# One more seven-product gate/up group ahead of the pairs, in place of a plain one, in a two-layer encoder on one core

## What is computed

```python
x = x + 0.5 * swiglu(rmsnorm(x, norm_ffn), w_gate, w_up, w_down)      # D_FF = 2816

def swiglu(h, w_gate, w_up, w_down):
    return (jax.nn.silu(h @ w_gate) * (h @ w_up)) @ w_down
```

## Time and profile before

| | us |
|---|---|
| Median of 3 runs | 2633.71 (2633.64 to 2634.29) |
| The profiled execution, its own time | 2634.64 |
| Its span in the trace | 2632.8 |
| TensorE busy | 2619.0 (99% of the span) |
| VectorE busy | 1881.9 (71%) |
| ScalarE busy | 1097.5 (42%) |
| GpSimd busy | 239.9 (9%) |
| The 16 DMA engines, main queue | 31.8% of the span |

### The profile page before, as it was taken

The page is one execution under the profiler, slowest core; times in us unless marked ns, Lnnn a source line. Parts: engine busy times, 40 slices in busy tenths (PEclk is TensorE's granted clock), DMA queues, the critical chain, the costliest instruction groups (busy, mean ns, idle before and its releaser), DMA issues.

```text
span 2632.8 us, 38540 instructions
## 1 busy us (share of the span) xinstructions
PE 2619.0 (99%) x14658; PEld 2306.5 (88%) x14658; DVE 1881.9 (71%) x2462; ACT 1097.5 (42%) x1561; POOL 239.9 (9%) x143
## 2 busy tenths in 40 slices
PE   8999999999999999999999999999999999999999
PEld 6899998888888888999988999888888888889998
DVE  8788865564665467888878888664755644689887
ACT  5343444454543233443433434444544522333333
POOL 2512100000000000211001111000000000001110
PEclk9999999999999999999999999999999999999999
DMA  7433233233224333333223332432322333324331
GB/s 239 124 104 96 80 128 101 81 93 95 83 66 144 100 106 99 111 113 104 88 81 112 96 104 71 153 92 64 115 82 80 100 116 98 115 80 137 96 96 56
DMA packets 293325, 269.70 MB, mean 102 GB/s; under 512 B 14036, under 2 KB 272513, under 8 KB 292685
## 3 DMA queue, kind: packets, MB, share of 16 engines
q1 hardware_dynamic: 288072, 259.09, 31.8%
q0 software_dynamic: 4512, 5.04, 0.7%
q10 hardware_dynamic: 646, 4.31, 0.4%
HBM read 259.75 MB, written 13.28 MB: 104 GB/s over the span
## 4 chain that ended last, share of the span: by engine, by line
PE 89%; DVE 5%; issue 2%; ACT 2%; DMA 1%; POOL 0%; SPq 0%; DVEq 0%; ACTq 0%; POOLq 0%
PE proj L574 22%; PE proj L576 22%; PE proj L575 22%; PE acc L574 6%; PE acc L575 6%; PE acc L576 6%; DVE ring_lo L1566 1%; ACT ring_hi L1111 1%; PE acc L844 1%; DVE xs L1592 1%; DVE work L1733 1%; DMA raw<-in_ffn_down 1%; PE acc L783 0%; DVE y_lo L1596 0%; DVE work L1580 0%
## 5 line engine op out<-in xcount | busy, mean ns | idle before, releaser
L574 PE MATMUL proj<-h_hi,ring_hi 128*128 128x512 f32 (+1 forms) x1664 | 572.1, 344 | 0.9 <-DVE work L1620 0.8
L576 PE MATMUL proj<-h_hi,ring_lo 128*128 128x512 f32 (+1 forms) x1664 | 567.2, 341 | 0.0
L575 PE MATMUL proj<-h_lo,ring_hi 128*128 128x512 f32 (+1 forms) x1664 | 566.8, 341 | 0.0
L574 PE MATMUL proj<-y_hi,ring_hi 128*128 128x256 f32 (+1 forms) x1376 | 427.1, 310 | 0.0
L576 PE MATMUL proj<-y_hi,ring_lo 128*128 128x256 f32 (+1 forms) x1376 | 426.8, 310 | 0.0
L575 PE MATMUL proj<-y_lo,ring_hi 128*128 128x256 f32 (+1 forms) x1376 | 426.7, 310 | 0.0
L574 PEld LDWEIGHTS proj<-h_hi,ring_hi 128*128 128x128 f32 x1664 | 316.1, 190 | 37.2 <-issue 1.7
L1111 ACT ACTIVATE ring_hi<-raw 128x1024 fp32r<-128x1024 f32 (+1 forms) x175 | 223.9, 1281 | 299.1 <-PE acc L576 210.5
L576 PEld LDWEIGHTS proj<-h_hi,ring_lo 128*128 128x128 f32 x1664 | 315.8, 190 | 35.7
L575 PEld LDWEIGHTS proj<-h_lo,ring_hi 128*128 128x128 f32 x1664 | 316.2, 190 | 33.7
L1566 DVE TENSOR_TENSOR ring_lo<-raw,ring_hi 128x1024 fp32r<-128x1024 f32 (+1 forms) x176 | 296.6, 1688 | 48.7 <-ACT ring_hi L1111 48.2
(11 more groups left out here) (276 smaller groups left out, 3876.3 us busy)
## 6 DMA issues: line engine op xcount, KB each, us to landing
raw<-in_ffn_gate SPq DMA_DIRECT2D x88, 512.0 KB, 3.9
raw<-in_ffn_up SPq DMA_DIRECT2D x88, 512.0 KB, 4.2
raw<-in_w_in SPq DMA_DIRECT2D x136, 256.0 KB, 3.6
raw<-in_w_in SPq DMA_DIRECT2D x60, 512.0 KB, 4.7
raw<-in_ffn_down SPq DMA_DIRECT2D x56, 512.0 KB, 4.4
work<-in_ffn_down SPq DMA_DIRECT2D x32, 512.0 KB, 6.1
raw<-in_w_out SPq DMA_DIRECT2D x16, 512.0 KB, 4.1
raw<-in_w_ret_o SPq DMA_DIRECT2D x12, 512.0 KB, 3.8
```

The costliest lines, as they stand in the source:

```text
L574: pe.matmul(o, s_hi, m_hi, start=start, stop=False)
L575: pe.matmul(o, s_hi, m_lo, start=False, stop=False)
L576: return pe.matmul(o, s_lo, m_hi, start=False, stop=stop)
```

## The change

Only groups 0 and 1 stay plain. Group 2 becomes a seven-product group by itself (the *odd* group) that runs directly after the down product of group 0, with ring slots 4, 5, 0, 1, 4, 5, 0, while slots 2 and 3 are kept for down weights; the down product of groups 1 and 2 follows it (`down_odd`). The operand sums and all seven operand splits move ahead of it, the residual adds of down 0 and `ups(1, 6)` move behind them on VectorE, and TensorE waits for both plain up tiles' scaling before the first product, as the products use all four `PB` banks. GpSimd starts its differences one group sooner. The load of the second down weights goes to its own place and waits for the last operand split. In every fast group, odd or in a pair, the last three products now accumulate in PSUM on top of the first ones in their banks: two VectorE additions (`gate_lo`, `v_sum`) and one ScalarE copy (`c5_copy`) fall away, product 6 waits for the third sum in place of the copy, and the next group's product 0 waits for the low silu product, which reads the bank directly. Pairs are still four, of groups 3 to 10.

```diff
 GRP = 256
 GROUPS = D_FF // GRP
-PLAIN = 3
+PLAIN = 2
 ITEMS_PAIR, TILES_PAIR = 2 * PROD + 2, 2 * PROD + 8
-PAIR_ITEM, PAIR_TILE = 3 * PLAIN, 4 * PLAIN + 16
+ODD_ITEM, ODD_TILE = 5, 16
+OP_ORDER = (S1, S3, N2, S4, A11, A12, A22)
 PRODUCTS = ((0, A11), (1, S1), (3, S3), (2, N2), (0, A12), (3, A22), (1, S4))
+ADDED = 4
...
-                after(5)
-                whole(0, 3)
-                after(6)
-                whole(1, 3)
-                after(7)
-                down_rows(l, f, 2)
+                sp.wait_ge(op_lo_ready, 7 * (2 * l + f) + 7)
+                down_rows(l, f, 2, 1)
+                for piece, which, half in ((1, 0, 0), (2, 1, 0), (5, 0, 1), (6, 1, 1)):
+                    after(ODD_ITEM + piece)
+                    gate_up(l, f, which, half, 3)
...
+                first = ffn_item(l, f) + LO_CREDIT + ODD_ITEM
                 if F4 == 0:
                     pool.wait_ge(decay_out, 16)
                 else:
-                    pool.wait_ge(weights_lo, I0)
-                for n in range(FAST):
-                    edges(n, I0 + ITEMS_PAIR * ((n - 1) // 2) + PROD * ((n - 1) % 2))
+                    pool.wait_ge(weights_lo, first)
+                edges(0, 0)
+                edges(1, first)
+                for n in range(2, FAST):
+                    edges(n, I0 + ITEMS_PAIR * ((n - 2) // 2) + PROD * (n % 2))
...
+                def group(F, item, slots, bank3_free, bank2_free):
+                    free = ((silu_lo_ready, F + FREE), (c12_done, F + FREE), bank3_free, bank2_free,
+                            (c1_copied, F + 1), (u3_done, F + 1), (c22_done, F + 1))
+                    for j, (bank, op) in enumerate(PRODUCTS):
+                        pe.wait_ge(*free[j])
+                        product(item + j, slots[j], PB[bank], op, j >= ADDED)
...
+                    group(F, I, slots[:PROD], (ffn_x, 8 * added + 6), (ffn_x, 8 * added + 5))
+                    group(F + 1, I + PROD, slots[PROD:], (c21_done, F + 1 + FREE), (u2_done, F + 1 + FREE))
                     down_pair(I + 2 * PROD, i, 2)
...
-                gate(5, 4, 2)
-                split_done(6)
-                up(0, 2, 0)
-                up(0, 2, 1)
-                down_two(7, 1, 1, 2)
-                pe.wait_ge(op_lo_ready, 7 * F4 + 7)
-                pe.wait_ge(ffn_x, 8 * (DOWNS * F4 + 2) + 6)
+                pe.wait_ge(gate_scaled, 2 * (c0 + 1) + 4)
+                pe.wait_ge(up_scaled, 2 * (c0 + 1) + 4)
+                for j, (bank, op) in enumerate(PRODUCTS):
+                    pe.wait_ge(op_lo_ready, 7 * F4 + OP_ORDER.index(op) + 1)
+                    if j >= ADDED:
+                        pe.wait_ge((c1_copied, u3_done, c22_done)[j - ADDED], FAST * F4 + 1)
+                    product(ODD_ITEM + j, ODD_SLOTS[j], PB[bank], op, j >= ADDED)
...
                 sigmoids(1)
-                whole(0, 2, 4, 6)
+                odd_hi(0, 6)
                 for n, op in enumerate((S1, S3, N2, S4)):
                     operand_hi(op, (s_ready, 4 * F4 + n + 1))
-                whole(1, 2, 0, 8)
+                odd_hi(1, 6)
+                for op in (A11, A12, A22):
+                    operand_hi(op, (tiles_done, T0 + 8 + FIRST_CREDIT))
+                odd_hi(2, 8)
+                odd_hi(3, 8)
                 hidden_his(1)
-                down_hi(1, 2, 16)
-                sigmoids(2)
-                down_hi(2, 4, 18)
-                hidden_his(2)
-                for op in (A11, A12, A22):
-                    operand_hi(op, (tiles_done, T0 + 20 + FIRST_CREDIT))
-                piece_hi(0, 0, 0, -8)
-                piece_hi(0, 0, 1, -8)
+                F, q = FAST * F4, g0 + PLAIN
+                act.wait_ge(gated_ready, 2 * (c0 + 2))
+                c1_copy(F, ODD_TILE)
+                odd_hi(4, ODD_TILE + 1)
+                odd_hi(5, ODD_TILE + 2)
+                odd_hi(6, ODD_TILE + 3)
+                down_hi(1, ODD_TILE)
+                sigmoid_lo(F, q, ODD_TILE)
+                second_hi(1, ODD_TILE + 6)
+                sigmoid_hi(F)
+                hidden_hi(q, 1, 0)
+                hidden_hi(q, 1, 1)
+                pair_hi(0, 0, 0, -8)
+                pair_hi(0, 0, 1, -8)
...
+                def sums(F, tile):
+                    done(T0 + tile + 3)
+                    dve.wait_ge(c1_copied, F + 1)
+                    dve.tensor_tensor(u2, c1, PB[2][:, :], ALU.add).then_inc(u2_done, 1)
+                    dve.wait_ge(u2_done, F + 1 + FREE)
+                    dve.tensor_tensor(u3, u2, PB[3][:, :], ALU.add).then_inc(u3_done, 1)
+                    dve.wait_ge(u3_done, F + 1)
+                    dve.tensor_tensor(c22, u3, PB[1][:, :], ALU.add).then_inc(c22_done, 1)
+
+                def gate_hi(F, tile):
+                    done(T0 + tile + 5)
+                    dve.wait_ge(c22_done, F + 1)
+                    dve.tensor_tensor(c21, u2, PB[3][:, :], ALU.add).then_inc(c21_done, 1)
+
+                def silu_low(F):
+                    dve.wait_ge(sig_lo_ready, F + 1)
+                    dve.tensor_tensor(silu_lo, PB[0][:, :], silu_lo, ALU.mult).then_inc(silu_lo_ready, 1)
...
+                def up_lo(F, tile):
+                    done(T0 + tile + 6)
+                    dve.wait_ge(c21_done, F + 1 + FREE)
+                    dve.tensor_tensor(c12, u2, PB[1][:, :], ALU.add).then_inc(c12_done, 1)
...
-                    def sums(g):
-                        F = FAST * F4 + 2 * i + g
-                        done(T0 + B + PROD * g + 3)
-                        dve.wait_ge(c1_copied, F + 1)
-                        dve.tensor_tensor(u2, c1, PB[2][:, :], ALU.add).then_inc(u2_done, 1)
-                        dve.wait_ge(u2_done, F + 1 + FREE)
-                        dve.tensor_tensor(u3, u2, PB[3][:, :], ALU.add).then_inc(u3_done, 1)
-                        dve.wait_ge(c5_copied, F + 1)
-                        dve.wait_ge(u3_done, F + 1)
-                        dve.tensor_tensor(v_sum, u2, c5, ALU.add).then_inc(v_done, 1)
-                        dve.wait_ge(v_done, F + 1)
-                        dve.tensor_tensor(c22, u3, c5, ALU.add).then_inc(c22_done, 1)
-
-                    def gate_lo(g):
-                        done(T0 + B + PROD * g + 4)
-                        dve.wait_ge(u2_done, FAST * F4 + 2 * i + g + 1 + FREE)
-                        dve.tensor_tensor(c11, c1, PB[0][:, :], ALU.add).then_inc(c11_read, 1)
-
...
@@ -1736,46 +1750,55 @@
                 ups(0, 2)
                 lo(4, 2, 2048, raw[:, 2, :])
                 gates(1, 4)
-                lo(5, 4, 2048, raw[:, 0, :])
+                F, q = FAST * F4, g0 + PLAIN
                 dve.wait_ge(xn_ready, 8 * (F4 + 1))
                 dve.tensor_tensor(s_acc, xn21, xn22, ALU.add).then_inc(s_ready, 1)
                 dve.wait_ge(s_ready, 4 * F4 + 1)
                 dve.tensor_tensor(xn21, xn11, xn21, ALU.subtract).then_inc(s_ready, 1)
                 operand_lo(0, S1)
                 dve.tensor_tensor(s_acc, xn11, s_acc, ALU.subtract).then_inc(s_ready, 1)
-                add_down(0, 8, 0)
                 operand_lo(1, S3)
-                add_down(0, 8, 1)
                 dve.wait_ge(s_ready, 4 * F4 + 3)
                 operand_lo(2, N2)
-                add_down(0, 8, 2)
                 dve.tensor_tensor(s_acc, xn12, s_acc, ALU.add).then_inc(s_ready, 1)
-                add_down(0, 8, 3)
-                lo(6, 0, 2048, raw[:, 1, :])
-                for m in range(4, 6):
-                    add_down(0, 8, m)
+                odd_lo(0)
                 dve.wait_ge(s_ready, 4 * F4 + 4)
                 operand_lo(3, S4)
-                for m in range(6, KT):
-                    add_down(0, 8, m)
-                ups(1, 6)
-                lo(7, 2, 2048, raw[:, 2, :])
-                gates(2, 16)
-                lo(8, 4, 2048, raw[:, 2, :])
-                ups(2, 18)
+                odd_lo(1)
                 operand_lo(4, A11)
                 for m in range(4):
-                    add_down(1, 20, m, PLAIN_BANKS)
+                    add_down(0, 8, m)
                 operand_lo(5, A12)
                 operand_lo(6, A22)
-                add_down(1, 20, 4, PLAIN_BANKS)
+                add_down(0, 8, 4)
+                add_down(0, 8, 5)
+                t2(F)
+                add_down(0, 8, 6)
+                odd_lo(2)
+                add_down(0, 8, 7)
+                odd_lo(3)
+                t4(F, q)
+                ups(1, 6)
+                for j in (4, 5, 6):
+                    odd_lo(j)
+                sums(F, ODD_TILE)
+                lo(ODD_ITEM + PROD, 2, 2048, raw[:, 2, :])
+                silu_low(F)
+                gate_hi(F, ODD_TILE)
+                hidden_hi(F, q)
+                lo(ODD_ITEM + PROD + 1, 4, 2048, down_second)
+                up_lo(F, ODD_TILE)
+                hidden_lo(F)
+                y_low(q, 1, 0)
+                y_low(q, 1, 1)
                 piece_lo(0, 0, 0)
                 piece_lo(0, 0, 1)
```

(61 more changed lines are left out.)

239 lines of the change are left out of this document (100 added, 139 removed).

## The result

The changed kernel takes **2715.42 us** (median of 6 runs, 2714.16 to 2718.48) against 2633.74 (6 runs, 2633.64 to 2634.29) of the kernel before: ratio 1.031, 95% interval 1.0299 to 1.0321. It is slower by 81.7 us, and the forecast was 2715.5. Its profiled execution took 2714.72 us, with a span of 2712.9.

What follows compares the result with a forecast made beforehand. TensorE, busy 99% of the span, was taken as the bound, so feeding it one group sooner was the question. Terms -6.4 - 3.1 + 42.7 + 38.6 - 2 + 12 = +81.8 us on 2634.64 gave 2716.4, median 2715.5; range 2692 to 2731.

Steps and rivals of the forecast that it cites:

- Matmul time: Seven products in place of a plain group's matmuls: 1.61 us less per feed-forward, four times, -6.4 us.
- Old waits gone: TensorE's waits ahead of the second down half and inside the first pair go, with their restarts: -3.1 us.
- VectorE's order: Feed-forwards two to four: TensorE waits 6.5 us inside down 0 and 7.7 ahead of product 0, together +42.7 us.
- The GpSimd block of the gating products: GpSimd's differences slow VectorE's gating products, so the operand chain begins at 2323.85; the other bound was about 2320.5.
- The first feed-forward: GpSimd's differences come after its table DMAs, so TensorE stands some 30 us inside down 0: +38.6 us.
- The DMA gap: GpSimd's 17.43 us between two DMA issues shrinks as one 1 MB load leaves: -2 us, bounds 0 and -17.4.
- The clock: Matmuls run slow for 5 us behind each of eight new stalls: +12 us, bounds 0 and 18.
- At no cost: Fast groups: fewer VectorE and ScalarE steps gain nothing; product 0's wait on the low silu product costs nothing.
- The clock stays up: Rival: no slow clock behind the stalls, everything else as forecast; 2703.5 us, chance 0.12.
- GpSimd's queue did not come free early: Denies the rival that GpSimd's first feed-forward queue frees early, 17.4 us less in place of 2; 2700, chance 0.06.
- The pairs have no new waits: Denies the rival of half-microsecond waits in each pair on low silu product and third sum; 2723.5, chance 0.05.
- The rival on the other side: Ahead of product 0, VectorE's operand work hides within down 0, so only the first two terms count; 2624.2, chance 0.03.

Runs made afterwards that it cites:

- e7: Against experiment 6: GpSimd's first-pair differences wait for the odd group's low hidden part, one VectorE piece moves behind four residual adds; 2626.72 us, ratio 0.9971.
- Experiment 3: Changed kernel with the first four residual adds of down 0 put back between the operand steps; 2709.30 us, ratio 1.0281.
- experiment 6: Changed kernel with VectorE's and ScalarE's head work ordered by due time, up-scaling wait ahead of product 2, two GpSimd differences on VectorE; 2637.07 us, ratio 1.0014.
- Experiment 1: Changed kernel with GpSimd's two differences in the first feed-forward issued ahead of the last table transfer; 2692.07 us, ratio 1.0216.
- experiment 4: Changed kernel with TensorE filling both waits with matmuls of no use into a free bank; 2705.36 us, ratio 1.0266.

## Why the prediction was right, point by point

The mechanism was right: where TensorE stands, what it waits for, and that the clock falls. That the total is right to 0.1 us is luck. The sum was made for the profiled execution, and there it gave 2716.4 where 2714.72 was measured; the changed kernel's median then lies 0.7 above its profiled execution, not 0.9 below. Within the sum, errors of both signs cancel. The heads of feed-forwards two to four grew by 42.1 us where the terms make 44.8. That of the first grew by 39.8 where they make 38.0. The rest of the kernel shrank by 1.8 in place of 1.0.

- **Matmul time, -6.4.** Right. The seven products take 20.16 us where nothing waits, as in e7, the double down 21.79, and the pairs run gapless. e7 gives this term without the others: its heads of feed-forwards two to four are 2.0, 2.1 and 2.5 us shorter than before, of which 1.6 each are the matmuls and the rest the old waits. Its first is 0.5 us longer, as 1.7 us of waits on adds are left there.
- **Old waits gone, -3.1.** Right: neither is in the list of waits any more. By the timelines they are worth 1.9 us in the heads and up to 1.8 in the rest.
- **VectorE's order, +42.7.** Right, with its two places. In the fourth feed-forward add 0 was forecast to begin 11.3 us after down 0's start (2323.85 + 12.8 against 2325.36) and began 11.25 us after it. Product 0 was forecast 25.1 us after the start (25.9 with the clock's share) and began 25.34 after it. The wait inside down 0 was to be 6.5 us and is 6.4 by the timeline. Ahead of product 0 it was to be 7.7 less the slow down, and is about 6. The GpSimd block of the gating products (taken, not the other bound) happened: 4.53 us for two. What it alone costs was not tried. Experiment 3 shows that the two waits are in series on one queue, as the prediction said, and experiment 6 that the amount of VectorE's work does not make them, for VectorE has two differences more to do there.
- **The first feed-forward, +38.6.** Product 0 was forecast at 109.0 and came at 109.39; the first pair at 150.9 and came at 153.49. 2.1 us of that 2.6 are products at the slow clock (22.21 us in place of 20.16), a term of its own there. Experiment 1 confirms the cause for 23 us of it.
- **The DMA gap, -2.** Wrong, by its whole size: 17.33 us against 17.43, with one load of 1 MB less beside it (between 49 and 65 us the DMAs move 269 GB/s in place of 304). So that load does not lengthen the gap. What GpSimd waits for there was not tried.
- **The clock, +12.** The mechanism was right, the size about 2 us too high: 10.1 measured by experiment 4, 9.5 by its heads. The length of the slow stretch was taken as 5 us where the matmuls show 3.5 to 4.6, so the products lose 1.9 us each and not 2.2. Behind the first wait 0.8 us was to come through in each feed-forward; in the later three it is 0.3 on average. The doubt from the printed clock of 1.00 is settled too, for the profile of after prints 0.67 to 0.90 in these stretches.
- **At no cost.** Right for the pairs: the new waits on the low silu product and the third sum do not appear.

The rivals fall with this. "The clock stays up" (2703.5) is refuted by the pitch of 0.21 us and by experiment 4. GpSimd's queue did not come free early. The pairs have no new waits. The rival on the other side, in which the operand work hides, did not happen in this order, but experiments 6 and 7 show what it takes: not the 11 us fewer of VectorE steps that the prediction asked for, but another order of the same steps and of two more, over a longer stretch. Its forecast time, 2624.2, is within 2.5 us of what e7 reaches. The prediction had seen both conditions, GpSimd's differences sooner and the second up scaling sooner, but took the up scaling's place ahead of product 0 as given.

## What to carry to other kernels

When a step is moved ahead of another, walk the queue of the engine that feeds it in its written order and ask of every waiting instruction what stands ahead of it. The change lost 81.7 us not by more work but because adds and scalings that free banks came to stand behind operands that were needed later, and weight differences behind table transfers. Ordering the feeding engines by the due times of their results, with one wait and GpSimd's differences moved, turned a 3.1% loss into a 0.3% gain. Put a wait at the first instruction that needs it and not at the head of the group: that alone was 27.8 us. Look at the first pass of a loop by itself: only there did GpSimd's queue still hold the table transfers, and that was 23.4 us.

## What the runs showed of the hardware that was not expected

- **Extra work saved time.** 52 matmuls in two waits of about 6 us (and 154 in the first feed-forward's) made the changed kernel 10.1 us faster, as the granted clock no longer fell in the later three feed-forwards and only for seven matmuls in the first.
- **GpSimd holds up some VectorE instructions and not others.** Beside a GpSimd difference, low parts with both operands in SBUF took 2.26 to 2.30 us in place of 0.7 (e6), while residual adds with one operand in PSUM took 0.68 to 0.69 (e6, e7). The Trainium skill (SBUF — State Buffer, SBUF: two separate sides) says that the two engines share a port pair as an exclusive lock, which a VectorE operation with two SBUF inputs takes against a GpSimd operation that reads SBUF. These rows agree. GpSimd is held too: its difference that began 0.6 us into a VectorE split with both operands in SBUF took 3.96 us in place of 2.4 (e6). Experiment 7 is worth 10.4 us by the choice of what runs beside GpSimd.
- **GpSimd's 17 us without an issue** between two table transfers stayed as it was when SyncE had one load less. When two differences were put into the gap (e1), the eighth transfer still came 16.5 us after the seventh, so they cost it nothing that the rows show. What ends the gap stays open.
